# A long fp32 network on one core: the rows of two following stages turned in the feed-forward tails, and attention's index projections in three float32r passes

## The reference, cut to what matters

```python
x = layernorm(ALPHA * x + (1 + gt2) * swiglu(x * (1 + sc2) + sh2), g, b)   # end of a feed-forward stage
# attention
hin = x * (1 + sc1) + sh1
proj = hin @ w_in        # 1024 query, 128 latent, 512 index-query, 64 index-key, 8 index-weight columns
s = einsum('bthd,bsd->bths', q_idx, k_idx)
score = einsum('bth,bths->bts', w_idx, relu(s))     # causal, the best 128 keys of each token are kept
# hybrid
h = rmsnorm(x, g_norm1) * (1 + sc1) + sh1
z = h @ w_in             # glu_a, glu_b, q, k, v, o, i_pre, f_pre, g_a, g_b
```

## Time and profile before

| | |
|---|---|
| median of 3 runs | 2736.38 us (2735.71 to 2737.82) |
| the profiled execution | 2738.78 us |
| its span | 2737.0 us |
| mean granted TensorE clock | 0.968 of full speed |
| TensorE matmul busy | 2538.3 us, 93% of the span |
| VectorE busy | 2035.8 us, 74% |
| ScalarE busy | 1067.4 us, 39% |
| GpSimd busy | 382.2 us, 14% |

### The profile page before, as it was taken

How to read it: one execution, slowest core, us unless ns; L and a number is a source line. 1 busy time by engine, 2 the same in 40 slices (tenths; PEclk the granted TensorE clock), 3 DMA queues, 4 the chain that set the end, 5 groups by cost and what they waited for, 6 DMA issues and landing times. The chain is left out here.

```text
span 2737.0 us, 43084 instructions
## 1 busy us (share of the span) xinstructions
PE 2538.3 (93%) x17291; PEld 2015.3 (74%) x17291; DVE 2035.8 (74%) x2894; ACT 1067.4 (39%) x1425; POOL 382.2 (14%) x207
## 2 busy tenths in 40 slices
PE   5999888889999989998999989999998999999993
PEld 3785888777888844467788867887578788888883
DVE  6872666687777628777877666986746999999994
ACT  2631244522220022543222004333223777777772
POOL 1000000000000020000000000000002356665551
PEclk8999999999999999999999998999998999999997
DMA  6221122336663280205665323321407899999983
GB/s 210 77 87 41 65 80 80 125 112 212 186 190 116 85 273 32 77 32 154 212 187 169 116 78 106 93 79 45 154 1 268 328 372 371 371 369 363 361 302 127
DMA packets 247595, 458.89 MB, mean 168 GB/s; under 512 B 31157, under 2 KB 205917, under 8 KB 232089
## 3 DMA queue, kind: packets, MB, share of 16 engines
q1 hardware_dynamic: 227384, 432.37, 45.4%
q0 software_dynamic: 14384, 24.25, 2.6%
q10 hardware_dynamic: 5682, 0.20, 0.1%
HBM read 456.24 MB, written 30.56 MB: 178 GB/s over the span
## 5 line engine op out<-in xcount | busy, mean ns | idle before, releaser
L49 PE MATMUL ffn_bank<-ffn_xT_high,ffn_wi_high 128*128 128x512 f32 x704 | 275.5, 391 | 5.5 <-DVE stay_z_r L43 3.1
L50 PE MATMUL ffn_bank<-ffn_xT_low,ffn_wi_high 128*128 128x512 f32 x704 | 275.2, 391 | 0.0
L3436 POOL DMA_INDIRECT expert_rows<-exp_ys,exp_to_row x32 | 153.8, 4805 | 45.2 <-issue 44.4
L49 PEld LDWEIGHTS ffn_bank<-ffn_xT_high,ffn_wi_high 128*128 128x128 f32 x704 | 132.5, 188 | 33.6 <-DVE stay_z_r L43 3.9
L50 PEld LDWEIGHTS ffn_bank<-ffn_xT_low,ffn_wi_high 128*128 128x128 f32 x704 | 132.3, 188 | 28.2
L43 DVE TENSOR_TENSOR moe_u_low<-moe_u,exp_u_high 128x4096 fp32r<-128x4096 f32 x32 | 141.6, 4425 | 12.8 <-ACT exp_u_high L3510 12.6
L43 DVE TENSOR_TENSOR moe_g_low<-moe_g,moe_g_high 128x4096 fp32r<-128x4096 f32 x32 | 141.6, 4425 | 8.5 <-ACT moe_g_high L3510 8.2
L43 DVE TENSOR_TENSOR moe_d_low<-moe_d,exp_d_high 128x4096 fp32r<-128x4096 f32 x32 | 141.4, 4419 | 0.0
L51 PE MATMUL ffn_bank<-ffn_xT_high,stay_z_r 128*128 128x512 f32 x352 | 139.8, 397 | 0.0
L51 PE MATMUL ffn_bank<-ffn_wo_high,ffn_act_low 128*128 128x512 f32 x352 | 138.0, 392 | 0.0
L49 PE MATMUL ffn_bank<-ffn_wo_high,ffn_act_high 128*128 128x512 f32 x352 | 137.7, 391 | 0.0
(11 more groups left out here) (730 smaller groups left out, 6726.9 us busy)
## 6 DMA issues: line engine op xcount, KB each, us to landing
moe_g<-in_w_e_gate SPq DMA_DIRECT2D x32, 2048.0 KB, 9.5
moe_u<-in_w_e_up SPq DMA_DIRECT2D x32, 2048.0 KB, 10.0
moe_d<-in_w_e_down SPq DMA_DIRECT2D x32, 2048.0 KB, 9.3
ffn_nw<-in_ada_w SPq DMA_DIRECT2D x24, 1024.0 KB
ffn_nw<-in_w_ada SPq DMA_DIRECT2D x24, 1024.0 KB
stay_z<-in_ffn_w_in SPq DMA_DIRECT2D x44, 512.0 KB, 5.1
ffn_wi<-in_ffn_w_in SPq DMA_DIRECT2D x44, 512.0 KB, 5.2
chunks_ada<-in_ada_w SPq DMA_DIRECT2D x16, 1024.0 KB, 5.3
```

Source lines behind the costliest of these rows:

```text
L49: nc.tensor.matmul(out, w[0], x[0], start=start, stop=False, **kw)
L50: nc.tensor.matmul(out, w[0], x[1], start=False, stop=False, **kw)
L3436: nc.gpsimd.indirect_dma_start(ys_dram, bass.IndirectOffsetOnAxis(ap=to_row[h][:, 0, 1:2].bitcast(U32), axis=0), ys[h][:, :], None, bounds ...
```

## The change

In each feed-forward tail the rows of the next stage are turned: tile 0 ahead of TensorE's group (3,0), tiles 1 to 3 after its last group. ffn0 transposes x; ffn1 multiplies by a diagonal of the reciprocal RMS, which needs square, root, reciprocal and diagonal in every tile. ScalarE evicts tiles 0, 1 and the first half of tile 3, VectorE tile 2 and the second half of tile 3. The result is handed on as hT; both following stages lose their own turning and evictions and begin with fillers (24 and 36). In attention the operand and the index weights are split and the five index jobs take three passes; the bias loads wait for the last index-query job, with gt, g and b behind them. In the hybrid the opening begins with the first half of block 0 (job 1 two pieces behind job 0), the vectors are turned after it, jobs 2 and 3 stand ahead of the gate job, low(1) and low(2) ahead of the chain, and gt and norm_g load after job 7. `first_high` and `wb_highs` release VectorE's two halves of block 0; the renamed semaphores and the re-placed tiles are left out below.

```diff
+                def turn(t):
+
+                    pe.wait_ge(s["normed"] if squares is None else s["diag_done"], t + 1)
+                    for k in range(KD):
+                        if squares is None:
+                            last = nc.tensor.transpose(turned_at(t, k), x[:, t, k:D:KD], ident[:, :])
+                        else:
+                            last = nc.tensor.matmul(turned_at(t, k), x[:, t, k:D:KD], diag[:, t, :], start=True, stop=True, skip_group_check=True)
+                        if k % 4 == 3:
+                            last.then_inc(s["turn_psum"], 1)
                 for t, j in ((1, 1), (2, 0), (2, 1), (3, 0), (3, 1)):
+                    if t == LAST and j == 0:
+                        turn(0)
                     for f in range(STEADY, NF):
                         down(f, t, j)
+                for t in range(1, NT):
+                    turn(t)
 
...
+                def take_turned(t, first, count):
+
+                    for k in range(first, first + count):
+                        act.wait_ge(s["turn_psum"], 2 * t + k // 4 + 1)
+                        nc.scalar.activation(next_rows(t, k), turned_at(t, k), ACT.Identity, bias=sh[:, k:k + 1], scale=sc[:, k:k + 1]).then_inc(s["turned"], 1)
                 for t in range(NT):
                     act.wait_ge(s["var_done"], t + 1)
                     nc.scalar.activation(rstd[:, t:t + 1], mv[:, t, 1:2], ACT.Sqrt).then_inc(s["root"], 1)
-                    if squares is not None and t:
-                        act.wait_ge(s["normed"], t)
-                        if t > 1:
-                            act.wait_ge(s["squared"], t - 1)
-                        nc.scalar.activation(sil[:, :, :].rearrange("p a t -> p (a t)"), x[:, t - 1, :], ACT.Square, accum_out=squares[:, t - 1:t]).then_inc(s["squared"], 1)
+                    if t > 1:
+                        act.wait_ge(s["affine_done"], 1)
+                        take_turned(t - 2, 0, KD)
+                    if squares is not None:
+                        act.wait_ge(s["normed"], t + 1)
+                        if t:
+                            act.wait_ge(s["squared"], t)
+                        col = squares[:, t:t + 1]
+                        nc.scalar.activation(sil[:, :, :].rearrange("p a t -> p (a t)"), x[:, t, :], ACT.Square, accum_out=col).then_inc(s["squared"], 1)
+                        act.wait_ge(s["squared"], t + 1)
+                        act.wait_ge(s["eps_done"], 1)
+                        nc.scalar.activation(col, col, ACT.Sqrt, scale=1.0 / D, bias=stay["eps"][:, :]).then_inc(s["mean_root"], 1)
+                take_turned(LAST, 0, KD // 2)
...
+                def diagonal(t):
+
+                    col = squares[:, t:t + 1]
+                    dve.wait_ge(s["mean_root"], t + 1)
+                    link(nc.vector.reciprocal(col, col))
+                    nc.vector.tensor_scalar(diag[:, t, :], ident[:, :], col, None, ALU.mult).then_inc(s["diag_done"], 1)
+
+                def between(t):
+                    if squares is not None and t:
+                        diagonal(t - 1)
+
+                def take_turned(t, first, count):
+
+                    for k in range(first, first + count):
+                        dve.wait_ge(s["turn_psum"], 2 * t + k // 4 + 1)
+                        nc.vector.tensor_scalar(next_rows(t, k), turned_at(t, k), sc[:, k:k + 1], sh[:, k:k + 1], ALU.mult, ALU.add).then_inc(s["turned"], 1)
...
+                              s["var_done"], s["root"], s["normed"], between=between)
+                dve.wait_ge(s["affine_done"], 1)
+                take_turned(LAST - 1, 0, KD)
+                if squares is not None:
+                    diagonal(LAST)
+                take_turned(LAST, KD // 2, KD // 2)
...
+        if between is not None:
+            between(t)
...
-                pool.dma_start(gt[:, :], spread(gate)).then_inc(s["v_loaded"], 16)
-                pool.dma_start(g[:, :], spread(ln_g)).then_inc(s["v_loaded"], 16)
-                pool.dma_start(b[:, :], spread(ln_b)).then_inc(s["v_loaded"], 16)
+                pool.wait_ge(s["job_done"], number[("qidx", 3)] + 1)
-                pool.wait_ge(s["h_done"], KD)
+                pool.dma_start(gt[:, :], spread(gate)).then_inc(s["tail_loaded"], 16)
+                pool.dma_start(g[:, :], spread(ln_g)).then_inc(s["tail_loaded"], 16)
+                pool.dma_start(b[:, :], spread(ln_b)).then_inc(s["tail_loaded"], 16)
...
-                for k in range(KD):
-                    for t in range(NT):
-                        last = nc.tensor.transpose(bank[k][:, t * P:(t + 1) * P], x[:, t, k:D:KD], ident[:, :])
-                    last.then_inc(s["xT_psum"], 1)
-                pe.wait_ge(s["h_done"], KD)
+                keep_busy(nc, bank[6], ident, 24)
...
-                            pe.wait_ge(s["kidx_loaded"], 32)
-                            out, lhs, rhs = bank[n % 4][:, :], w_kidx[:, k, :, :].rearrange("p a i -> p (a i)"), hT[:, k, :]
+                            pe.wait_ge(s["index_split"], 1)
+                            pe.wait_ge(s["h_split"], k + 1)
+                            out = bank[n % 4][:, :]
+                            halves = tuple(v[:, k, :, :].rearrange("p a i -> p (a i)") for v in (w_kidx_high, w_kidx_low))
                         elif name == "qidx":
-                            pe.wait_ge(ring_loaded[0], 16)
+                            out = bank[n % 4][:, :]
+                            halves = tuple(v[:, k, q * P:(q + 1) * P] for v in (w_qidx_high, w_qidx_low))
                         else:
-                        last = nc.tensor.matmul(out, lhs, rhs, start=(k == 0), stop=(k == KD - 1))
+                        if name in ("kidx", "qidx"):
+                            last = matmul_halves(nc, out, halves, (h_high[:, k, :], h_low[:, k, :]), start=(k == 0), stop=(k == KD - 1))
+                        else:
+                            last = nc.tensor.matmul(out, lhs, rhs, start=(k == 0), stop=(k == KD - 1))
...
-                for k in range(KD):
-                    act.wait_ge(s["xT_psum"], k + 1)
-                    nc.scalar.activation(hT[:, k, :], bank[k][:, :], ACT.Identity, bias=sh[:, k:k + 1], scale=sc[:, k:k + 1]).then_inc(s["h_done"], 1)
...
+                def qidx_high(q):
+                    cols = slice(q * P, (q + 1) * P)
+                    nc.scalar.copy(w_qidx_high[:, :, cols], ring(0)[:, :, cols]).then_inc(s["index_high"], 1)
+
+                act.wait_ge(s["kidx_loaded"], 32)
+                nc.scalar.copy(w_kidx_high, w_kidx[:, :, :, :]).then_inc(s["index_high"], 1)
                 for t in range(NT):
                     take("tok", t, ckv[:, t, :], slice(0, LATENT), signal=False)
                     take("tok", t, widx[:, t, :], slice(LATENT, LATENT + IDX_HEADS), scale=IDX_HEADS ** -0.5 * IDX_DIM ** -0.5)
+                act.wait_ge(ring_loaded[0], 16)
+                qidx_high(0)
                 act.wait_ge(s["rms_in"], NT)
                 nc.scalar.activation(rms[:, :], rms[:, :], ACT.Sqrt).then_inc(s["rms_root"], 1)
+                for q in range(1, 4):
+                    qidx_high(q)
...
-                dve.wait_ge(s["v_loaded"], 16 * 5)
-                link(nc.vector.tensor_scalar(gt[:, :], gt[:, :], 1.0, None, ALU.add))
+                for k in range(KD):
+                    nc.vector.tensor_copy(h_high[:, k, :], hT[:, k, :]).then_inc(s["h_highs"], 1)
+                    dve.wait_ge(s["h_highs"], k + 1)
+                    low_half(nc.vector, h_low[:, k, :], hT[:, k, :], h_high[:, k, :]).then_inc(s["h_split"], 1)
+                dve.wait_ge(s["index_high"], 1)
+                low_half(nc.vector, w_kidx_low[:, :, :, :], w_kidx[:, :, :, :], w_kidx_high).then_inc(s["index_split"], 1)
+
+                def qidx_low(q):
...
                 for t in range(NT):
                     dve.wait_ge(s["act_took"], t + 1)
                     link(nc.vector.tensor_tensor_reduce(relu[:, 0, 0:LATENT], ckv[:, t, :], ckv[:, t, :], 1.0, 0.0, ALU.mult, ALU.add, rms[:, t:t + 1]))
                     nc.vector.tensor_scalar(rms[:, t:t + 1], rms[:, t:t + 1], 1.0 / LATENT, 1e-6, ALU.mult, ALU.add).then_inc(s["rms_in"], 1)
+                qidx_low(0)
                 dve.wait_ge(s["rms_root"], 1)
                 link(nc.vector.reciprocal(rms[:, :], rms[:, :]))
                 for t in range(NT):
...
+                dve.wait_ge(s["tail_loaded"], 16 * 3)
+                link(nc.vector.tensor_scalar(gt[:, :], gt[:, :], 1.0, None, ALU.add))
...
-                pool.dma_start(gt[:, :], spread(gate)).then_inc(s["v_loaded"], 16)
-                pool.dma_start(norm_g[:, :], spread(w["m_norm_g"])).then_inc(s["v_loaded"], 16)
+                pool.wait_ge(s["job_done"], 8)
+                pool.dma_start(gt[:, :], spread(gate)).then_inc(s["late_loaded"], 16)
...
-                pe.wait_ge(s["rows_loaded"], 16 * 6)
...
+                def opening(q, k):
+
```

(63 more changed lines are left out.)

128 lines of the change are left out of this document (60 added, 68 removed).

## The result

The changed kernel took 2742.85 us, the median of 19 runs (2736.73 to 2752.3), where the kernel before took 2736.38 in as many runs beside it (2730.55 to 2740.86). The ratio is 1.0028, with a 95% interval of 1.0018 to 1.0037: some 5 to 10 us slower. The forecast was 2735.3 (2729.5 to 2741.5).

A forecast was written before the change was run, and what follows sets the result against it. TensorE, busy 93% of the span, was taken as the bound. First seam -3.6 and second seam +2.5 gave -1.1 us (-5.5 to +3.5), so 2735.3 us by the median, range 2729.5 to 2741.5.

The forecast's parts named there:

- The first seam: ffn0's tail into attention: terms summed to -3.6 us (-4.9 to -1.5).
- attention's start: First seam: token jobs start 6.9 instead of 8.2 us after attention's start, 1.3 us won.
- the weights' wait of 1.0: First seam: index jobs wait for split key and query weights, 1.0 us (bounds 0 to 2.7).
- Rival D: Attention's index jobs: three passes save nothing, bound by their 24 weight loads; +5.5, 2740.8 us; chance 0.03.
- The second seam: ffn1's tail into the hybrid mixer: terms summed to +2.5 us (-0.6 to +5).
- Step 1: Second seam, ffn1's tail: reciprocals, diagonals, evictions and eight products add 7.5 us (6.2 to 8.2).
- Step 2: Second seam: the hybrid's opening begins 8.6 instead of 12.7 us after the stage's start, 4.1 us won.
- Step 3: Second seam: the hybrid's opening takes 12.0 instead of 14.06 us, 2.1 won (0 to 3).
- Steps 4 and 5: Hybrid: 12 small vector transposes between matmuls cost +1.2 us; the 2.24 us stall moves two jobs later, nothing won.
- Rival B: Hybrid: late VectorE becomes the bound, TensorE waits at each of three blocks; 8 us, 2743.3 us; chance 0.14.
- Rival C: Token jobs and hybrid's opening: fillers do not warm the clock; +1.7 and +2.1, 2739.1 us; chance 0.05.
- rival A: Both seams at their good ends: early weights, warm tail, opening and restart; -7.2, 2729.2 us; chance 0.24.

The follow-up runs named there:

- first seam alone: Changed kernel, but with ffn1's tail and the hybrid of the kernel before; 2730.48 us, 0.9976 to 0.9996 of before.
- before again: The kernel before, unaltered, run once more for a second profile; 2730.68 us (1 run).
- more fillers: Changed kernel with 80 fillers instead of 36 at the hybrid's start; 2745.86 us, 1.0026 to 1.0054 of before.
- all four edits: Changed kernel with ffn1's rows multiplied on VectorE and transposed, row loads later, block 3 split early, 56 fillers; 2738.59 us, 0.9997 to 1.0020 of before.
- scaled rows: Changed kernel, but in ffn1's tail VectorE multiplies rows by the reciprocal RMS and TensorE transposes them; 2742.93 us, 1.0016 to 1.0040 of before.

## Why the prediction was wrong

The first seam was forecast at -3.6 and cost -3.8 in the trace, -4.8 in its own run. Its terms: VectorE's evictions 3.92 for 3.3; attention's start 6.7 for 6.9; index jobs as said; the weights' wait of 1.0 did not come. That the sum hit so well is partly luck: the whole tail of ffn0 cost only 2.7 in that profile (2.7 to 3.9 in the others), and the 1.0 that was not needed was made up for by the 1.6 lost behind the logits. Rival D (three passes save nothing) fell; its price was also added wrongly, since -1.1 + 6.6 on 2736.4 is 2741.9 and not 2740.8.

The second seam was forecast at +2.5 (bounds -0.6 to +5) and cost +7.2 in the trace and +10.5 in its own run. The mechanism was the one I had, a longer tail against an earlier opening; two steps were mis-sized.

- **Step 1, the tail of ffn1, +7.5.** It cost 11.3. The price of a product came from the token jobs, whose operand is contiguous; it measured 0.48 and not 0.235. And I counted only the last tile's eight: the eight that the edit puts ahead of (3,0), and the sixteen behind (3,1), I costed at nothing by the first seam's cover of 6.8 us, where they are transposes. They made VectorE wait 1.98 + 0.66 + 0.48 = 3.1 us. With transposes in their place the tail measured +7.9, and with products at the contiguous price +7.4, without these waits: the price is the error, and the uncounted products cost something only at the true one.
- **Step 2, the opening's start, -4.1.** It measured -1.2. I took the landing of 6.8 us from before and looked for relief from the rows no longer loaded; I did not ask which loads move *forward* when ScalarE's square and root go. Those six loads are visible in the code right behind the root. The relief did not come either: without the spread rows, and with the six loads out of the way, the block landed in 6.6 us.
- **Step 3, a warm opening, -2.1.** 12.8 us for 12.0, against 14.1, 12.7, 11.3 and 12.8 in the four profiles with before's hybrid: the 14.06 of the one trace was an unlucky value, so there was less to win. The fillers ended 5 us too early to matter.
- Steps 4 and 5 held: the vectors cost 1.0 (1669.8 to 1670.75) for 1.2, and the stall stood ahead of job 6 with 2.26 us.

In the two profiles these steps add up: +11.3 - 1.2 - 1.3 + 1.0 is 9.8, and 17 jobs into the hybrid TensorE stands 10.0 us further behind ffn1's first instruction than before (511.7 us against 501.7). The trace's total of 7.2 is smaller because the profile of before is 2.8 us longer behind that point: 4.1 longer in the gated heads (65.2 us against 61.2) and 1.3 shorter elsewhere. The forecast's bounds were also narrower than its own steps allow: their upper ends add up to +7.6, not +5.

Rival B named the time (2743.3), but its mechanism did not come: between 1701 and 1861 TensorE waits for no split. Rival C, that fillers don't warm the clock, is refuted: the granted clock reached 1.00 over 1650.43 to 1651.43, where TensorE had done nothing but fillers since the stage's start, and the run with 80 held it; the rule of the Trainium skill (TensorE: Matmul & The Clock Gate, Part 4: PE-mode transpose), that transposes do not count as work for the clock, is not what these runs show. Of rival A's ingredients the early key and query weights came; the warm opening came only with the row loads moved or more fillers.

I had called 0.2% the resolution and taken one profile of before as its time by stages. Its ffn1 to routing was 797.3, where the same code gave 790.3 to 797.0 elsewhere, so the second seam's real cost is nearer 10 us than 7.

## What to carry to other kernels

When an edit deletes the first instructions of an engine's program, look at what moves up behind them: DMA issues that had stood a microsecond behind a critical load now stand beside it. Price a matmul by the layout of its stationary operand as well as by its shape, and count every group that the edit inserts, also those that end before the stage's critical engine. And where a stage's ends are at a wait of a few microseconds, take two profiles of the kernel before: here its ffn1 to routing took 797.3 and 793.8 us, and the difference lay in the opening and in the restart behind the stall.

## What the runs showed of the hardware

The part of the hybrid with four gated heads, the same code in all kernels, took from 61.1 to 67.1 us in different profiles. The windows view of it in the first seam alone, before again, and more fillers:

```profile
1834.64:1896.36 61.72, 56.95 (x272) 43.44 (x272) 35.11 (x76) 21.71 (x26) 0.00 (x0) 0.97 0.17 52
```

```profile
1838.88:1904.15 65.27, 59.30 (x272) 46.09 (x272) 37.18 (x85) 22.86 (x28) 0.00 (x0) 0.92 0.16 49
```

```profile
1851.20:1918.26 67.06, 60.89 (x272) 46.60 (x272) 37.22 (x85) 22.86 (x28) 0.00 (x0) 0.90 0.16 48
```

The length goes with the granted clock (0.97, 0.92, 0.90), and TensorE is busy 56.95 to 60.89 us with the same 272 records; the two long profiles have a wait of 4.0 and 4.4 us for VectorE in them, with records at 1.2 GHz behind it. What decides between the two is not shown. It is not chance from one execution to the next alone: the two profiles of before agree (65.2 and 65.3 us), and so do the two of the changed kernel (61.1 and 61.2). A saving of a few us upstream can be lost there, as with all four edits. It does not explain scaled rows, whose 3.4 us were kept to routing; why its times don't show them stays open.
